# Expert results added into a DRAM stream by gather and scatter instead of a combine stage

## What is computed

```python
g_idx = jnp.argmax(g_logits, axis=-1)                # one of 4 groups for each token
e_sel = ...                                          # the 4 expert logits of that group
top_v, top_i = lax.top_k(e_sel, 2)                   # two experts of the group
top_w = jax.nn.softmax(top_v, axis=-1) * g_p
expert_id = g_idx[:, None] * 4 + top_i
...
a = jax.nn.silu(hg) * hu * gates[..., None]          # 16 SwiGLU experts, 1024 -> 256 -> 1024
y = jnp.einsum('tef,efd->td', a, w_down)
x = x + y
out = rmsnorm(x, g_final)
```

## Time and profile before

| | |
|---|---|
| median of three runs | 1076.79 us (1074.95 to 1082.03) |
| profiled execution | 1083.94 us, its span 1080.7 us |
| PE busy | 943.3 us (87% of the span) |
| DVE, ACT, POOL busy | 431.6, 368.4, 128.6 us |
| moved by DMA | 181.4 MB, 168 GB/s over the span |
| routing, experts, combine | from about 668, 738 and 1025 us |

### The profile page before, as it was taken

The page is one execution under the profiler, slowest core; times in us unless marked ns, Lnnn a source line. Parts: engine busy times, 40 slices in busy tenths (PEclk is TensorE's granted clock), DMA queues, the critical chain, the costliest instruction groups (busy, mean ns, idle before and its releaser), DMA issues. The chain is left out here.

```text
span 1080.7 us, 13980 instructions
## 1 busy us (share of the span) xinstructions
PE 943.3 (87%) x4765; PEld 764.4 (71%) x4765; DVE 431.6 (40%) x524; ACT 368.4 (34%) x544; POOL 128.6 (12%) x159
## 2 busy tenths in 40 slices
PE   6996999999999999989999997926999999989500
PEld 5785888888888676558888885715888887768400
DVE  4673212121211234232222232375646567675056
ACT  6762012111111123221122222503656567665212
POOL 0011000000001000000000001202112111211074
PEclk8997999999999999998999999965999999999855
DMA  9891101111005966544000102932587878993177
GB/s 384 329 297 60 49 1 39 40 40 40 20 20 210 408 262 279 203 182 161 1 1 1 29 1 76 331 118 79 196 309 260 307 260 317 341 337 131 69 268 259
DMA packets 37534, 181.38 MB, mean 168 GB/s; under 512 B 4268, under 2 KB 8748, under 8 KB 26811
## 3 DMA queue, kind: packets, MB, share of 16 engines
q1 hardware_dynamic: 26706, 141.57, 35.3%
q0 software_dynamic: 6864, 24.68, 7.2%
q10 hardware_dynamic: 3888, 14.16, 3.2%
HBM read 147.59 MB, written 40.78 MB: 174 GB/s over the span
## 5 line engine op out<-in xcount | busy, mean ns | idle before, releaser
L1634 DVE TENSOR_TENSOR Wl<-raw,Wh x48 | 109.9, 2292 | 72.9 <-ACT Wh L1574 72.8
L1574 ACT CAST Wh<-raw x48 | 91.6, 1911 | 55.4 <-issue 53.8
L1481 PE MATMUL ps<-Wh,e_xTh 128*128 x216 | 87.2, 404 | 4.0 <-issue 4.0
L551 PE MATMUL ps<-f_win_h,f_hTh 128*128 128x512 f32 x216 | 86.6, 401 | 0.6 <-DVE f_hTl L443 0.6
L1482 PE MATMUL ps<-Wl,e_xTh 128*128 x216 | 84.9, 393 | 0.0
L553 PE MATMUL ps<-f_win_l,f_hTh 128*128 128x512 f32 x216 | 84.8, 393 | 0.0
L1483 PE MATMUL ps<-Wh,e_xTl 128*128 x216 | 84.8, 393 | 0.0
L552 PE MATMUL ps<-f_win_h,f_hTl 128*128 128x512 f32 x216 | 84.5, 391 | 0.0
L1556 POOL DMA_INDIRECT e_xg<-h_rows,idx x28 | 46.7, 1669 | 247.0 <-PE ps L1666 199.3
L1481 PE MATMUL ps<-f_rg_h,f_cTh 128*128 128x512 f32 x144 | 56.7, 394 | 0.0
L1483 PE MATMUL ps<-f_rg_h,f_cTl 128*128 128x512 f32 x144 | 56.2, 390 | 0.0
(11 more groups left out here) (303 smaller groups left out, 1811.5 us busy)
## 6 DMA issues: line engine op xcount, KB each, us to landing
raw<-in_w_e SPq DMA_DIRECT2D x48, 1024.0 KB, 6.8
y_rows<-e_y ACTq DMA_DIRECT2D x27, 512.0 KB, 5.4
t_ring<-in_kc SPq DMA_DIRECT2D x8, 1024.0 KB, 12.5
t_ring<-in_vc SPq DMA_DIRECT2D x8, 1024.0 KB, 8.7
f_win_raw<-in_w_in SPq DMA_DIRECT2D x3, 2048.0 KB, 22.8
f_xin<-in_x SPq DMA_DIRECT2D x9, 512.0 KB, 3.6
x_rows<-f_xin SPq DMA_DIRECT2D x9, 512.0 KB, 2.6
y_rows<-in_x SPq DMA_DIRECT2D x1, 4608.0 KB, 19.8
```

What stands on the lines that cost most here:

```text
L551: pe.matmul(ps[:, bank, :], hTh[:, c, :], win_h[i][:, c, :], start=(c == 0), stop=False)
L1481: pe.matmul(out, xh, wh, start=(n == 0), stop=False)
L1574: act.copy(Wh[q][:, ds(off, PIECE)], raw[q][:, ds(off, PIECE)]).then_inc(hi_ok[q], 1)
L1634: dve.tensor_tensor(Wl[q][:, ds(off, PIECE)], raw[q][:, ds(off, PIECE)], Wh[q][:, ds(off, PIECE)].bitcast(F32), ALU.subtract).then_inc(lo_ ...
```

## The change

The results are no longer kept by place. A copy of the stream, `acc_rows`, lies in DRAM. For each expert tile POOL gathers the tile's rows of it into one of four slots (the first four tiles of X serve as ring), DVE adds the two halves of y from PSUM onto them, and POOL scatters them back. The weight of a row (`GATE`, by place) goes into the gating product. The experts are renumbered: place in the group first, then group, so that any four neighbours belong to four groups and no row can be in two of them; gather j therefore waits for scatter j-4 only. Empty places get an index beyond the last row, and the transfers skip them. The last tile's result and index go through buffers of their own. After the last scatter SP reloads the stream into X, and square, factor (in four groups), scaling and store follow in the experts block itself. The copies into `y_rows`, `POS` and the combine block are gone; `xg` has three buffers and is cleared once.

Routing, SP and POOL:

```diff
+            for n in range(NT):
+                sp.dma_start(acc_dram[n * P:(n + 1) * P, :], X[:, n, :]).then_inc(keep["acc_st"], 16)
...
             pool.memset(ones[:, :], 1.0).then_inc(ones_ok, 1)
+            pool.memset(keep["xg"][:, :, :], 0.0)
```

Routing, PE and DVE:

```diff
-                last = pe.matmul(ps[:, 5, 0:NTILE], big[:, i, :], A[:, i, :], start=(i == 0), stop=(i == K2 - 1))
+                last = pe.matmul(ps[:, 5, 0:2 * NTILE], big[:, i, :], A[:, i, :, :].rearrange("p a n -> p (a n)"),
+                                 start=(i == 0), stop=(i == K2 - 1))
...
-                for g in range(EG):
-                    last = v(M[:, k, :, g * EE:(g + 1) * EE], H[:, k, :, :],
-                             G1[:, :, g:g + 1].to_broadcast([P, NT, EE]), ALU.mult)
+                last = v(M[:, k, :, :].rearrange("p t (e g) -> p t e g", g=EG), bcast4(H[:, k, :, :], EG),
+                         G1[:, :, :].rearrange("p t (o g) -> p t o g", o=1).to_broadcast([P, NT, EE, EG]), ALU.mult)
...
+            v(WTr[:, :, :], WT[:, :, :], tok[:, 1, :].rearrange("p (o n) -> p o n", o=1).to_broadcast([P, 2, NT]), ALU.mult)
-            then(dve.scalar_tensor_tensor(out=pf[:, :], in0=tt[:, :], scalar=float(P), in1=rr[:, :], op0=ALU.mult,
-                                          op1=ALU.add))
-            then(dve.tensor_copy(POS[:, :], pf[:, :]))
...
-                last = v(A[:, k * NT:(k + 1) * NT, :], A[:, k * NT:(k + 1) * NT, :], bcast(tok[:, 0, :], NTILE), ALU.mult)
+                own = slice(k * NT, (k + 1) * NT)
+                then(v(A[:, own, 0, :], A[:, own, 1, :], bcast(tok[:, 0, :], NTILE), ALU.mult))
+                last = v(A[:, own, 1, :], A[:, own, 1, :], bcast(WTr[:, k, :], NTILE), ALU.mult)
...
             dve.wait_ge(idx_ps, 1)
-            dve.tensor_copy(IDX[:, :], ps[:, 5, 0:NTILE])
+            dve.tensor_copy(GATE[:, :], ps[:, 5, NTILE:2 * NTILE])
+            then(dve.tensor_scalar(none[:, :], ps[:, 5, 0:NTILE], 0.0, pad[:, :], ALU.is_equal, ALU.mult))
+            then(dve.scalar_tensor_tensor(out=none[:, :], in0=none[:, :], scalar=-1.0, in1=ps[:, 5, 0:NTILE], op0=ALU.add,
+                                          op1=ALU.add))
+            then(dve.tensor_copy(IDX[:, :], none[:, :]))
+            then(v(none[:, :], none[:, :], last_tile[:, :], ALU.mult))
+            then(r(used[:, 0:1], none[:, :], AX_X, ALU.add))
+            dve.tensor_copy(keep["idx_last"][:, :], used[:, 0:1])
```

Experts, POOL (in place of the fetch alone):

```diff
+            def gather(j):
+                if j >= EG:
+                    pool.wait_ge(y_st, 16 * (j - EG + 1))
+                else:
+                    pool.wait_ge(acc_st, 16 * NT)
+                if j:
+                    pool.wait_ge(a_ld, 16 * j)
+                pool.indirect_dma_start(ring[:, j % 4, :], None, acc_dram[:, :],
+                                        bass.IndirectOffsetOnAxis(ap=IDX[:, j:j + 1], axis=0), bounds_check=NT * P - 1, oob_is_err=False).then_inc(a_ld, 16)
+            def scatter(j):
+                pool.wait_ge(y_ok, 2 * j + 2)
+                if j:
+                    pool.wait_ge(y_st, 16 * j)
+                pool.indirect_dma_start(acc_dram[:, :], bass.IndirectOffsetOnAxis(ap=IDX[:, j:j + 1], axis=0),
+                                        ring[:, j % 4, :], None, bounds_check=NT * P - 1, oob_is_err=False).then_inc(y_st, 16)
+            for j in range(XG):
+                fetch(j)
+            with ExitStack() as maybe:
+                for s in range(NTILE):
...
+                        fetch(s + XG)
...
+                    gather(s)
+                    if s >= 1:
+                        scatter(s - 1)
+            every, but_one = tail(pool, 2), sums(pool, 1)
+            pool.wait_ge(y_st, but_one)
+            pool.tensor_tensor(mark[:, 0:1], nhalf[:, :], nhalf[:, :], ALU.add)
+            pool.wait_ge(y_ok, every)
+            pool.tensor_tensor(mark[:, 1:2], nhalf[:, :], nhalf[:, :], ALU.add).then_inc(mark_ok, 1)
+            pool.wait_ge(mark_ok, 1)
+            pool.indirect_dma_start(acc_dram[:, :], bass.IndirectOffsetOnAxis(ap=keep["idx_last"][:, 0:1], axis=0), v_last,
+                                    None, bounds_check=NT * P - 1, oob_is_err=False).then_inc(y_st, 16)
```

Experts, ACT and DVE, and the end on SP:

```diff
-                    act.copy(y[:, par, 0:512], ps[:, 4, :]).then_inc(y_ok, 1)
-                    act.wait_ge(dn_ps, 2 * s)
-                    act.copy(y[:, par, 512:D], ps[:, 5, :]).then_inc(y_ok, 1)
...
-                    act.dma_start(y_dram[ds((s - 1) * P, P), :], y[:, par, :]).then_inc(y_st[par], 16)
...
-                dve.tensor_tensor(sg[:, :], sg[:, :], ps[:, 2 + like % 2, FE:2 * FE], ALU.mult).then_inc(a_ok, 1)
+                dve.scalar_tensor_tensor(out=sg[:, :], in0=sg[:, :], scalar=GATE[:, ds(s, 1)],
+                                         in1=ps[:, 2 + like % 2, FE:2 * FE], op0=ALU.mult, op1=ALU.mult).then_inc(a_ok, 1)
                 rest_of_piece(s + 2, (0,))
+                if like >= 1:
+                    dve.wait_ge(a_ld, 16 * s)
+                    for h in range(2):
+                        v, half = (s - 1) % 4, slice(h * 512, (h + 1) * 512)
+                        dve.wait_ge(dn_ps, 2 * s - 1 + h)
+                        dve.tensor_tensor(ring[:, v, half], ps[:, 4 + h, :], ring[:, v, half], ALU.add).then_inc(y_ok, 1)
...
+            sp.wait_ge(y_st, sums(sp, 0))
+            for t in range(NT):
+                sp.dma_start(X[:, t, :], acc_dram[t * P:(t + 1) * P, :]).then_inc(r_ld[t][0], 16)
+            for t in range(NT):
+                sp.wait_ge(o_ok, t + 1)
+                if t < TS:
+                    sp.dma_start(io["y_p"][t * P:(t + 1) * P, :], X[:, t, :]).then_inc(o_st[t % 3], 16)
+                else:
+                    sp.dma_start(io["y_s"], X[0:ROWS_S, t, :]).then_inc(o_st[t % 3], 16)
```

More of the change, by code:

```diff
@@ L1553, in fetch @@
             def fetch(j):
-                if j >= 2:
-                    pool.wait_ge(tr_ps, j - 1)
-                pool.indirect_dma_start(xg[:, j % 2, :], None, h_dram[:, :],
-                                        bass.IndirectOffsetOnAxis(ap=IDX[:, j:j + 1], axis=0)).then_inc(x_ld[j % 2], 16)
-            for j in range(NTILE):
-                if j <= MIN_TILES:
-                    fetch(j)
-                else:
-                    with pool.If(started(pool, j - 1) >= 1):
-                        fetch(j)
+                if j >= XG:
+                    pool.wait_ge(tr_ps, j - XG + 1)
@@ L1657, in _ @@
             tile_steps(dve, step)
+            slot, landed, done_by = last_slot(dve), sums(dve, 0), [tail(dve, 1 + h) for h in range(2)]
+            dve.wait_ge(a_ld, landed)
+            for h in range(2):
+                dve.wait_ge(dn_ps, done_by[h])
+                dve.tensor_tensor(v_last[:, h * 512:(h + 1) * 512], ps[:, 4 + h, :], flat_ring[:, ds(slot + h * 512, 512)],
+                                  ALU.add).then_inc(y_ok, 1)
+            dve.wait_ge(g_ld, G0 + 16)
+            for t in range(NT):
+                if t in FACTORS:
+                    dve.wait_ge(r_ok, 2 * SQ0 + 2 * FACTORS.index(t) + 2)
+                dve.scalar_tensor_tensor(out=X[:, t, :], in0=X[:, t, :], scalar=st[:, 4 * t + 2:4 * t + 3],
+                                         in1=gf[:, :], op0=ALU.mult, op1=ALU.mult).then_inc(o_ok, 1)
         @block.tensor
```

219 lines of the change are left out of this document (91 added, 128 removed).

## The result

The changed kernel takes 1053.38 us (median of four runs, 1051.84 to 1058.42), the kernel before 1078.64 (median of four, 1074.95 to 1082.03). The ratio is 0.9762, with a 95% interval of 0.9735 to 0.9790. The forecast was 1057.1 us with a range of 1048 to 1073. The profiled execution took 1054.81 us, its span is 1053.1.

What follows compares the result with a forecast made beforehand. The prediction took PE to bound the expert stage and a chain without PE the tail. -24.5 (tail) + 2 (experts) + 2.8 (routing) = -19.7 us off the median 1076.8 gave 1057.1 us, range 1048 to 1073.

Steps and rivals of the forecast that it cites:

- The tail: From the last product to the end: 59.7 us before, ending at 1056.2 after, a gain of 24.5 us.
- 9.18 MB through one pipe: Tail: SP's reloads, then stores, share one pipe at 345 GB/s, 26.6 us; 35.4 at 259 GB/s, 22.5 at 408.
- The margin of the norm: Tail: square, factor and three scalings behind the last load take 6 to 7 us, hidden under 9 us of older stores.
- Rival 2: Tail: the pipe runs at the old tail's 259 GB/s, 8.8 us more, 1066 in all; chance 0.06.
- The experts: Expert stage: DVE gains two adds of 0.68 per tile, ACT loses two copies; +2 us, within -1 to +8.
- a step in which three weight pieces fall needs 10.3 against PE's 9.33, where it was 8.9: Expert stage: DVE's work in us per such step, now with the adds, against PE's; five such steps.
- my lower bound: Expert stage: -1 us, if ACT was what was late; ACT has 1.2 us less in three-piece steps.
- issue: 9.7: Experts and tail: PE's longest wait, 9.7 us in 9 waits, 5.7 of it at the exit, which is not touched.
- The routing: Routing stage: selection, index and clearing terms sum to +2.8 us, bounds +1.5 to +11.
- Rival 1: Expert stage: DVE becomes the bound, 1 us for each of 16 experts, 1071 in all; chance 0.10.
- Rival 3: Expert stage: scatters form a chain; tiles pay landing beyond 9.33 us, 59 us at 11.5, 1116 in all; chance 0.08.
- Rival 4: Expert stage: GpSimd's issues hold DVE, 54 x 0.94 = 51 us, some hidden, 1057 to 1108, say 1083; chance 0.04.

Runs made afterwards that it cites:

- e8: The changed kernel with four of the eight stores of y_p left out, 2.1 MB of the tail's 9.2 MB: 1053.82 us, ratio 0.9755.
- e4: The changed kernel, but GpSimd clears xg after the last factor of the routing stage, not ahead of the first: 1054.04 us, ratio 0.9773.
- e2: The kernel before with only the new numbering of the experts, weights permuted alike and selection products made two: 1081.24 us, ratio 1.0017.
- e15: The kernel before with the new expert numbering and TensorE's register reads ahead of the transposes of sg: 1070.77 us, ratio 0.9901.
- e10: The changed kernel, but TensorE reads a step's registers ahead of the transposes of sg of the step before: 1045.05 us, ratio 0.9684.
- e13: The kernel before with TensorE's register reads of a step ahead of the transposes of sg of the step before: 1070.57 us, ratio 0.9909.
- e3: The changed kernel, but every scatter except the last tile's is sent twice, the second after the first has landed: 1149.83 us, ratio 1.0652.
- e12: The changed kernel with early register reads and the tail's norm factors in five groups instead of four: 1043.77 us, ratio 0.9654.
- e17: The changed kernel with early register reads, five groups of factors, and e_sg ahead of e_xTl on VectorE: 1046.17 us, ratio 0.9668.

## Why the prediction was right, step by step

**The sum.** Forecast -24.5 in the tail, +2 in the experts, +2.8 in the routing, 0 in the attention. By the profiled pair: 30.5 - 59.7 = -29.2, +4.1 and +3.0, together -22.1, against a difference of the medians of 25.3. Beyond these three stretches the profiled execution of the changed kernel was 5.5 us ahead when its routing began (663.5 against 669.0), all of it by 475 us, when the dropped copies began in the kernel before, and 3.1 by 355 us. Over the 14 profiles the routing begins at 664.3 to 669.0 us in the four kernels with the copies and at 662.6 to 666.7 in the ten without. A gain of up to 2 us from dropping them isn't excluded; the forecast zero stands within that.

**The tail** was right in its mechanism, and its gain came out 4.7 us larger than forecast. "9.18 MB through one pipe", loads ahead of stores and the norm under them, is what the changed kernel does: its transfers land one behind the other up to the end. The term that was mis-sized is the pipe's speed, 345 GB/s: once the queue is full, 0.524 MB land every 1.26 us, some 416 GB/s, and the window from 1032 to 1047 has 403, near the 408 that the prediction named and did not take. From 1027.12 to the end it is 25.98 us where 29.25 were counted; the second and third load land 1.6 and 2.4 us behind the one before, or it would be 1.5 less. The margin of the norm was thinner than it looked: its 7 us behind the last load came out as counted (7.03), but with the faster pipe they end only 0.7 us ahead of the queue, and e8, without a part of the stores, shows them as the end. The first part, from the last product to the whole stream in DRAM, took 4.55 us, not 5.9: the scatter landed 2.6 us after its issue, less than any of the fetches that stood for it. It carried 17 rows (in the trace, 17 packets of 4 KB), the fetches 128. Rival 2, 259 GB/s, falls.

**The experts** came out near the size, for another reason. +4.1 in the profiled pair, +1.9 to +4.1 with e4 and e8, against +2 within -1 to +8. The step that failed is "a step in which three weight pieces fall needs 10.3 against PE's 9.33, where it was 8.9", as the cause of what was late before. Those steps lose 1.1 us without any add (e2, e15) and in sum no more with them (e10). That ACT's half got shorter would explain it, and it was the reason for my lower bound, but no run takes ACT's share by itself. The other half of the lateness I did not see. I read "issue: 9.7" in the earlier trace rows as mostly the exit and left it aside as untouched; it stands for register reads and the branch behind them, which lie open where PE has had to wait, or nearly to wait, for e_sg. In steps 0 to 24 their edit is worth 4.5 us in the kernel before (e13) and 10.2 in the changed one (e10), so the change made such places more frequent: that is its loss in the expert stage, for with the early reads the two kernels' stages are 273.5 and 274.5 us.

**The routing** is +3.0 against +2.8, and the terms match less well than the sum. The index products with 64 columns cost nothing more (7.94 us for 36, against 7.89 in the earlier trace rows) where +1.0 was counted, and the operations behind them 1.4 us, as counted:

```profile
725.50 7.94 PE L1354 MATMUL ps<-r_A,r_big 128*128 128x64 f32 x36 [13.71 <-DVE r_A L1462]
...
733.55 0.19 DVE L1492 COPY gate<-ps 128x32 f32<-128x32 f32 x1 [2.18 <-PE ps L1354]
...
734.82 0.15 DVE L1499 CAST idx_last<-r_used 128x1 int32<-128x1 f32 x1
```

The clearing cost no more than the 0.3 counted (e4). What was counted too much there came back elsewhere: the ninth row began 1.4 us later than in the profile of before, 1.1 more than the clearing explains, and that place differs by 2.6 us between the ten profiles with the same routing. The routing as a whole takes 71.2 to 74.3 us in them, so that the sum met the forecast to 0.2 is in part luck.

**Rival 1** (DVE becomes the bound) falls: with the reads out of the way every step with fewer than three pieces takes 9.3 us in e10. **Rival 3** (the chain of scatters) was real and not reached: a link took 6.5 us in the middle and 6.8 in the mean, where the mean would have had to pass 9.33; e3 passed it and paid. The sign that the prediction gave for it, GpSimd waiting for a scatter in many tiles, did show, and alone means little: these 19 waits took 63.6 us of GpSimd's time (in total, times, longest) and PE waited for no fetch but the first.

```profile
POOL acc_rows L1637 <- DMA acc_rows<-x,idx: 39.1, 9, 7.0
POOL x L1630 <- DMA acc_rows<-x,idx: 24.5, 10, 6.6
```

**Rival 4** (DVE held by GpSimd) falls. The subtractions between 757 and 997 us (min/median/max in ns), beside up to three indirect issues per tile, against the 2279 to 2294 of the earlier trace rows:

```profile
L1723 DVE TENSOR_TENSOR Wl<-raw,Wh x45: 2280/2291/2294, 757.3 to 996.7; - x45
```

**A better version.** The early reads help both kernels; with them the changed one, with five groups of factors, takes 1043.77 us and the one before 1070.57. The gain of the change itself is the same in both settings: 25.3 us without the early reads, 25.5 with them (e10 against e13). The fifth group of factors, the only other difference of e12 from e10, is worth nothing that its runs can tell.

## What to carry to other kernels

A wait named "issue" is not a fixed cost: look at what an engine's sequencer must read or branch on right behind a semaphore wait, and move those reads ahead of the wait; here that was worth 8 to 10 us of either kernel's median, a third of what the whole change gained. Where a stage's end is both a queue of bytes and a chain of small operations, work out both up to the end: here they lie 0.7 us apart, so less bytes (e8) or a shorter chain (e12) alone gained nothing that could be told. Operations that follow each other without a listed wait need not set their own pace: hold their starts against the landings that they wait for. A read-modify-write through DRAM per tile is free as long as one link is in the mean shorter than the tile; find that margin first, because past it every tile pays.

## What the runs showed of the hardware

- Two register reads (0.30 us each at least) and a branch behind a wait that had only just ended opened a gap of 1.29 us on PE between two steps, of which the profile showed 0.86 as idle; ahead of the wait they left no gap.
- Loads and stores of 0.5 MB that SP issued landed in the order of their issue, one every 1.22 to 1.30 us while DMA was full (403 GB/s from 1032 to 1047).
- A wait of 0.78 us more on PE, right behind one of 0.99, was followed by 3.4 us at 1.2 GHz instead of 2.4 (e17 against e12).
- A scatter of 17 rows of 4 KB landed 2.6 us after its issue with DMA nearly idle. The others, of up to 128 rows, took 6.5 in the middle under a DMA share of 0.6 to 0.8 (11.9 at most). Its issue on GpSimd took 1.0 to 3.1 us.
- Small operations of GpSimd stretch beside DVE: 0.19 to 1.29 us and 0.58 to 1.47 during scalings with both inputs in SBUF. The Trainium skill (SBUF — State Buffer, Who interferes with whom) says that a DVE instruction with two SBUF inputs and a GpSimd instruction that reads SBUF exclude each other, and whoever issues first blocks the other. The runs agree with the half in which DVE goes first; the other half, DVE held by GpSimd, shows in none of the 45 subtractions above.
- The 36 passes of 128 x 128 weights took 7.94 us with 64 columns and 7.89 with 32.
